# The sample group's expert unit in the middle of the sequence on 128 doubled rows, and the last four up-row groups using the free down-row buffers too

## What the reference computes

```
def block(xb):
    qv = (xb @ w_query).astype(f32).reshape(PEER_BLOCK, PEER_HEADS, 2, PEER_DHALF)
    s = jnp.einsum('thsd,hskd->thsk', qv, keys)
    sv, si = lax.top_k(s, PEER_TOPK)
    cand = sv[:, :, 0, :, None] + sv[:, :, 1, None, :]
    ...
    g = jax.nn.softmax(fv, axis=-1)
    u = expert_down[eidx]
    act = jax.nn.gelu(jnp.einsum('thkd,td->thk', u, xb).astype(f32), approximate=False) * g
    v = expert_up[eidx]
    return jnp.einsum('thk,thkd->td', act.astype(v.dtype), v)
```

## Time and profile before

| | us |
|---|---|
| Median of 3 runs | 2483.84 (2475.89 to 2489.05) |
| The profiled execution, its own time | 2482.62 |
| Its span | 2480.7 |
| GpSimd busy (1154 instructions) | 1090.3 (44%) |
| VectorE busy | 1510.9 (61%) |
| TensorE busy | 1365.7 (55%) |
| Mean granted TensorE clock | 0.733 of full speed |

### The profile page before, as it was taken

The page is one execution under the profiler, slowest core; times in us unless marked ns, Lnnn a source line. Parts: engine busy times, 40 slices in busy tenths (PEclk is TensorE's granted clock), DMA queues, the critical chain, the costliest instruction groups (busy, mean ns, idle before and its releaser), DMA issues.

```text
span 2480.7 us, 19709 instructions
## 1 busy us (share of the span) xinstructions
PE 1365.7 (55%) x6380; PEld 764.8 (31%) x6380; DVE 1510.9 (61%) x3235; ACT 279.0 (11%) x575; POOL 1090.3 (44%) x1154
## 2 busy tenths in 40 slices
PE   4697997999644998556652222233233233233265
PEld 0276674878633845443320000000000000000010
DVE  0454998165688123777667776767776767676411
ACT  1011000111112002111110110000110001010000
POOL 0122000010130000476767777777777777777632
PEclk7798998999766999787866666655656665665555
DMA  9821000221332050799999999999999999999854
GB/s 367 315 64 52 34 34 0 87 73 37 94 94 93 2 189 26 296 365 403 409 403 409 409 406 409 409 406 405 406 401 396 409 409 405 408 403 407 279 145 152
DMA packets 209033, 651.98 MB, mean 263 GB/s; under 512 B 26192, under 2 KB 52464, under 8 KB 204793
## 3 DMA queue, kind: packets, MB, share of 16 engines
q0 software_dynamic: 150016, 545.33, 56.6%
q1 hardware_dynamic: 58092, 103.70, 11.8%
q10 hardware_dynamic: 824, 1.70, 0.2%
HBM read 643.24 MB, written 7.54 MB: 262 GB/s over the span
## 4 chain that ended last, share of the span: by engine, by line
DMA 21%; POOL 15%; issue 10%; PE 7%; DVE 7%; DVEq 0%; POOLq 0%; ACT 0%
DMA arena<-in_expert_up_dram,rows 16%; POOL arena L1675 8%; POOL arena L1659 7%; DMA arena<-in_expert_down_dram,expert 5%; PE ps L1797 4%; DVE arena L1903 2%; PE ps L1805 2%; DVE arena L1862 0%; DVE arena L1861 0%; PE ps L1344 0%; DVEq L1855 0%; DVE keys L1860 0%; DVE arena L1888 0%; DVE arena L1885 0%; DVE arena L1889 0%
## 5 line engine op out<-in xcount | busy, mean ns | idle before, releaser
L1797 PE MATMUL ps<-arena 128*32 128x512 f32 x2048 | 409.8, 942 | 831.1 <-DMA arena<-in_expert_up_dram,rows 831.1
L1903 DVE CUSTOM_DVE_ANT_0 arena<-arena,ps 128x1024 f32<-128x1024 f32 x512 | 617.1, 1219 | 317.0 <-DMA arena<-in_expert_down_dram,expert 301.7
L1675 POOL DMA_INDIRECT arena<-in_expert_up_dram,rows x512 | 490.6, 958 | 241.0 <-issue 136.4
L1659 POOL DMA_INDIRECT arena<-in_expert_down_dram,expert x528 | 501.3, 949 | 200.8 <-issue 155.8
L1797 PEld LDWEIGHTS ps<-arena 128*32 128x32 f32 x2048 | 81.9, 146 | 1120.1 <-issue 1120.0
L546 PE MATMUL ps<-arena 128*128 128x260 f32 x896 | 207.7, 391 | 14.8 <-ACT arena L477 7.8
L546 PEld LDWEIGHTS ps<-arena 128*128 128x128 f32 x896 | 173.0, 194 | 52.3 <-issue 16.2
L954 POOL MEMSET arena<- 128x528 f32 x2 | 1.1, 538 | 305.2 <-POOLq L2017 305.2
L1344 PE MATMUL ps<-arena 128*128 128x260 f32 x512 | 124.4, 404 | 4.9 <-POOL counting L1642 3.4
L1071 PE MATMUL ps<-arena 128*128 128x260 f32 x512 | 112.5, 383 | 0.0
L1344 PEld LDWEIGHTS ps<-arena 128*128 128x128 f32 x512 | 102.0, 202 | 28.9 <-issue 6.3
(11 more groups left out here) (347 smaller groups left out, 1878.4 us busy)
## 6 DMA issues: line engine op xcount, KB each, us to landing
arena<-in_w_ada_dram SPq DMA_DIRECT2D x12, 2048.0 KB
arena<-in_w_in_dram SPq DMA_DIRECT2D x11, 2048.0 KB, 8.4
arena<-in_expert_down_dram,expert POOLq DMA_INDIRECT x528, 12.6
arena<-in_w_ada_final_dram SPq DMA_DIRECT2D x4, 2048.0 KB
arena<-in_w_query_dram SPq DMA_DIRECT2D x8, 1024.0 KB, 16.4
arena<-in_expert_up_dram,rows POOLq DMA_INDIRECT x512, 12.1
out_dram<-arena SPq DMA_DIRECT2D x13, 512.0 KB, 2.9
arena<-in_x_prompt_dram SPq DMA_DIRECT2D x2, 2048.0 KB
```

The lines of the kernel that those rows point to most:

```text
L1659: G.indirect_dma_start(U[i][0:rows, :], None, down, bass.IndirectOffsetOnAxis(ap=idx[u % 2][0:rows, k:k + 1], axis=0))\
L1675: G.indirect_dma_start(Vr[j], None, up, bass.IndirectOffsetOnAxis(ap=at, axis=0))\
L1797: last = mm(ps[32 * j:32 * j + 32, c, :], Z[:, j, m, :], Vr[4 * half + j][:, c * 512:(c + 1) * 512], start=(p % 4 == 0 and m == 0), stop=( ...
L1903: V.tensor_tensor_reduce(U[i][0:rows, :], U[i][0:rows, :], row, 1.0, 0.0, ALU.mult, ALU.add, dots[g % 2][0:rows, j:j + 1]).then_inc(s_uuse ...
```

## The change

The sample unit becomes one step of 128 rows: the partitions 0 to 63 hold the 64 sample rows with the experts 0 to 7, and the partitions 64 to 127 the same rows with the experts 8 to 15. For that its scores and its rows are made on all 128 partitions (twice the matmuls in `score_samples`, wider ones in `samples`), and top-k's result is copied into an index tile `sample` of its own in two halves. The add has 8 experts with a weight of 128 rows by 8 columns instead of 16 with 64 rows. The sample unit is put between the token units 19 and 20 (step 40 of now 65), and its closing three units later. The up buffers get a second set, the first eight down buffers: of the last four up groups (61 to 64) the second and the fourth use it, and the first of these waits until all products are done. The rest renumbers steps, waits and closings accordingly.

The core of the diff:

```diff
-            last = nc.tensor.matmul(ps[0:64, 2 + t % 2, 0:NK], self.qpad[:, t, :], self.kT[:, t, :], start=(t < 2),
-                                    stop=(t >= 2 * PH - 2))
+            for r in (0, 64):
+                last = nc.tensor.matmul(ps[r:r + 64, 2 + t % 2, 0:NK], self.qpad[:, t, :], self.kT[:, t, :],
+                                        start=(t < 2), stop=(t >= 2 * PH - 2))
...
-    Vr = rows16[0:VR]
+    S = 2 * NU
+    units = list(range(NU))
+    units.insert(20, "samples")
+    steps = [S if u == "samples" else 2 * u + half for u in units
+             for half in range(1 if u == "samples" else 2)]
+    NSTEP = len(steps)
+    step_of = {g: n for n, g in enumerate(steps)}
+    unit_at = {g: (units.index("samples") if g == S else units.index(g // 2)) for g in steps}
+
     first_U, all_U = rows16[VR:] + more, rows16[VR:] + more + late
+    Vr = [rows16[0:VR], all_U[0:VR]]
...
-    groups = [("token", v) for v in range(2 * NU)]
-    groups[2 * NU - 2:2 * NU - 2] = [("sample", 0), ("sample", 1)]
-    at_step = {g: [g - LAG] for g in range(LAG, NSTEP)}
+    second = [n for n in range(NSTEP) if n >= NSTEP - LAG and (n - (NSTEP - LAG)) % 2]
+    at_step = {n: [n - LAG] for n in range(LAG, NSTEP)}
     at_step[NSTEP - 1] = list(range(NSTEP - 1 - LAG, NSTEP))
-    block_done = [2 * (16 * b + 16) + (4 if b == NB - 1 else 0) for b in range(NB)]
-    samples_done = 2 * 2 * NU
+    V_of = [1 if n in second else 0 for n in range(NSTEP)]
+    V_use = [1 + sum(V_of[m] == V_of[n] for m in range(n)) for n in range(NSTEP)]
+    V_before = [max([m for m in range(n) if V_of[m] == V_of[n]], default=None) for n in range(NSTEP)]
+    block_done = [2 * (step_of[16 * b + 15] + 1) for b in range(NB)]
+    samples_done = 2 * (step_of[S] + 1)
+    close_at = {units.index(PH * (b + 1) + 2): b for b in range(NB - 1)}
+    close_at[units.index("samples") + 3] = NB
+    closings = [close_at[u] for u in sorted(close_at)] + [NB - 1]
...
-                    G.indirect_dma_start(U[i][0:rows, :], None, down,
-                                         bass.IndirectOffsetOnAxis(ap=idx[u % 2][0:rows, k:k + 1], axis=0))\
+                    at = idxS[:, j:j + 1] if g == S else idx[u % 2][:, k:k + 1]
+                    G.indirect_dma_start(U[i], None, down, bass.IndirectOffsetOnAxis(ap=at, axis=0))\
...
+                g, r = steps[n], V_of[n]
+                if g != S and g % 4 == 0:
+                    pool.wait_ge(s_idxT, g // 4 + 1)
+                    pool.sem_inc(s_gatep, 1)
+                if r and V_before[n] is None:
+                    pool.wait_ge(s_uused, GATE * NSTEP)
                     pool.sem_inc(s_gatep, 1)
                 for j in range(VR):
-                    if j % 4 == 0 and n:
-                        pool.wait_ge(s_vused, 2 * (n - 1) + 1 + j // 4)
+                    if j % 4 == 0 and V_before[n] is not None:
+                        pool.wait_ge(s_vused, 2 * V_before[n] + 1 + j // 4)
                         pool.sem_inc(s_gatep, 1)
...
-                            k = GATE * v + 4 * half + j
+                            k = 4 * half + j
                             pe.wait_ge(s_sd, k + 1)
                             for c in range(2):
-                                last = mm(ps[0:NS, 2 + c, :], sdiag[0:64, k, :],
-                                          Vr[4 * half + j][0:64, c * 512:(c + 1) * 512],
-                                          start=(k == 0), stop=(k == 2 * GATE - 1))
+                                last = mm(ps[0:NS, 2 + c, :], sdiag[:, k, :], Vr[r][k][:, c * 512:(c + 1) * 512],
+                                          start=(k == 0), stop=(k == GATE - 1))
                     last.then_inc(s_vused, 1)
...
-                for n in at_step.get(g, ()):
-                    add(n)
+                if n >= LAG:
+                    add(n - LAG)
+                if g == S:
+                    continue
...
+                if units[i] == "samples":
+                    V.tensor_copy(idxS[0:64, :], ef[0:64, 0:GATE])
+                    done(V.tensor_copy(idxS[64:P, :], ef[64:P, GATE:TOPK]))
+                    dve.sem_inc(s_top, 1)
+                else:
+                    V.tensor_copy(idx[par], ef).then_inc(s_top, 1)
...
+            for i, u in enumerate(units):
+                if u == "samples":
+                    products(step_of[S])
+                    topk(i + 1)
+                    weight(step_of[S])
+                    continue
+                n, b = step_of[2 * u], u // PH
...
+                c = close_at.get(i)
+                if c is not None:
+                    k, rows, r = closings.index(c), NS if c == NB else P, c // NB
+                    if c == NB:
+                        close(k, samples_done, ps[0:NS, 2:4, :], NS, 1, x1[0:NS, NB * D:(NB + 1) * D])
+                    else:
+                        close(k, block_done[c], ps[:, 0:2, :], P, 0, x1[:, c * D:(c + 1) * D])
+                if i + 1 < len(units):
+                    topk(i + 1)
...
-            for g in (2 * NU, 2 * NU + 1):
-                products(g)
-                weight(g)
-            close(3, samples_done, ps[0:NS, 2:4, :], NS, 1, x1[0:NS, NB * D:(NB + 1) * D])
-            variance(3, NS)
-            normed(3, NS, 1)
```

More of the change, by code:

```diff
@@ L1544, in stage_peer @@
     yb = take(D)
-    x64 = take(D)
+    xs = take(D)
     late = [take(D) for _ in range(2)]
@@ L1550, in stage_peer @@
     Z = take(4, 8, 32)
-    sel64 = take(PH, NS, rows=NS)
-    r64 = take(NS)
+    sel = take(2 * PH, NS, rows=NS)
+    pick = take(NS)
     s_rep = take(2, NK)
@@ L1566, in stage_peer @@
     gel = [take(GATE) for _ in range(2)]
[L1567 removed]
+    acts = take(GATE)
+    sdiag = take(GATE, NS)
     stat, rstd = take(1), take(1)
@@ L1783, in add @@
             def add(n):
-                kind, v = groups[n]
-                p = v // 4
-                if kind == "token" and v % 4 == 0:
+                g, r = steps[n], V_of[n]
+                p = g // 4
+                if g != S and g % 4 == 0:
                     pe.wait_ge(s_Z, 4 * p + 4)
-                if kind == "token" and v % 16 == 0 and v:
-                    pe.wait_ge(s_blkrd, v // 16)
+                if g != S and g % 16 == 0 and g:
+                    pe.wait_ge(s_blkrd, closings.index(g // 16 - 1) + 1)
                 for half in range(2):
                     for j in range(4):
-                        pe.wait_ge(s_V[4 * half + j], 16 * (n + 1))
-                    if kind == "token":
-                        m = 2 * (v % 4) + half
+                        pe.wait_ge(s_V[r][4 * half + j], 16 * V_use[n])
+                    if g != S:
+                        m = 2 * (g % 4) + half
                         for c in range(2):
@@ L1813, in samples @@
                 pe.wait_ge(s_ssrd, 2)
-                nc.tensor.transpose(ps[0:64, 4, 0:NS], sel64.rearrange("p h b -> p (h b)"), ident[0:NS, 0:NS])
+                rows = sel.rearrange("p h b -> p (h b)")
+                nc.tensor.transpose(ps[:, 4, 0:NS], rows, ident[0:NS, 0:NS])
                 for j in range(2):
-                    last = mm(ps[0:64, 2 + j, :], sel64.rearrange("p h b -> p (h b)"),
-                              h2[0:NS, 4 * D + j * 512:4 * D + (j + 1) * 512], start=True, stop=True)
-                last.then_inc(s_ps64, 1)
+                    last = mm(ps[:, 2 + j, :], rows, h2[0:NS, 4 * D + j * 512:4 * D + (j + 1) * 512],
+                              start=True, stop=True)
+                last.then_inc(s_psx, 1)
             ask(2)
-            for g in range(NSTEP):
+            for n, g in enumerate(steps):
                 u, p = g // 2, g // 4
@@ L1847, in _ @@
                     turned(actT, actb[p % 2]).then_inc(s_actT, 1)
+            for n in range(NSTEP - LAG, NSTEP):
+                add(n)
         @block.vector
@@ L1863, in top16, with topk @@
                 V.max_index(index[:, 8:16], vals[:, 8:16], rep)
-            def topk(unit):
-                par = unit % 2
-                ef = efb[(unit // 2) % 2][:, unit % 2, :]
+            def topk(i):
+                par, unit = i % 2, units[i]
+                ef = efb[0][:, 0, :] if unit == "samples" else efb[(unit // 2) % 2][:, unit % 2, :]
+                unit = NU if unit == "samples" else unit
                 for s in range(2):
@@ new lines, in weight @@
+            def weight(n):
+                g = steps[n]
+                par = unit_at[g] % 2
+                dve.wait_ge(s_gelu, n + 1)
+                if g == S:
+                    tt(acts[0:64, :], gel[n % 2][0:64, :], w[par][0:64, 0:GATE], ALU.mult)
+                    tt(acts[64:P, :], gel[n % 2][64:P, :], w[par][64:P, GATE:TOPK], ALU.mult).then_inc(s_acts, 1)
+                else:
+                    if g % 4 == 0 and g >= 8:
+                        dve.wait_ge(s_actT, g // 4 - 1)
+                    u, half = g // 2, slice((g % 2) * GATE, (g % 2 + 1) * GATE)
```

(14 more changed lines are left out.)

196 lines of the change are left out of this document (84 added, 112 removed).

## The result

The changed kernel takes **2419.56 us** in the median of four runs (2417.09 to 2422.96), the kernel before 2480.39 us beside it (four runs, 2475.89 to 2489.05). The ratio of the times is 0.9752, with a 95% interval of 0.9725 to 0.978: 2.5% faster. Forecast were 2416 us, 2404 to 2435. Two later measurements of the same kernel gave 2417.41 and 2419.15 us, five runs each. The forecast took its start from a median of 2483.84 us for the kernel before; beside the changed kernel it measured 2480.39. So the time is 3.6 us off, but the change, -60.8 us where -68.1 were forecast, is 7.3 us off: half of that error is hidden by the start.

A forecast was written before the change was run, and what follows sets the result against it. The prediction took the DMA to bound the middle, with a slower, serial end. Its terms, -176.8+20.6+81.6+6+0.5 = -68.1 us, took 2483.8 us to 2416 us, range 2404 to 2435.

The forecast's parts named there:

- term 1: The old end, from issue of the last token down-gather at 2303.9 to 2480.7, is removed: -176.8 us.
- X: At the new end: the moment when issue of the last down group ends, from which the end is counted.
- Term 2: In the DMA-bound middle: one more full step, 16 sample gathers of 128 rows instead of 32 of 64: +20.6 us.
- Term 4: Behind the sample step: GpSimd waits 12.5 us for top-k, the queue covers 6.5, DMA idles: +6 us (0 to 8.4).
- Term 5: Sample add in the middle: 32 records in 15.3 us as the clock rises, nearly all hidden by the queue: +0.5 us.
- term 3: New end: group 61 waits for group 60's add, then 32 gathers follow, last add and closing: +81.6 us.
- Rival B: Sample gathers: duplicate rows still run at half rate, 20.6 us more, 2436 us; chance 0.05.
- rival C: At the end: the second buffer set brings nothing, a group costs 13.9 us, 11 us more, 2427 us; chance 0.06.
- rival D: Later units: top-k stays late, GpSimd stalls before each of 11 units, slower than before, 2508 us; chance 0.03.
- The rule that the prediction weighed: TensorE's clock: sustained matmuls release the throttle, only idling brings it back, whatever the rows; sample add then costs 0.5 us.
- Rival A: Sample add: TensorE stays at 1.2 GHz, GpSimd waits 6.4 and 8.7 us, +11.6 us, 2427 us; chance 0.27.

The follow-up runs named there:

- the experiment with 64 partitions: Changed kernel with the 16 sample gathers, down and up, cut to the first 64 of their 128 partitions, half the bytes: 2426.97 us.
- the kernel with the short add: Changed kernel leaving out three of four experts in each half of the samples' add, all gathers kept: 2418.89 us.
- the 64 rows: Changed kernel whose samples' add uses only the first 64 of the 128 rows of each gathered tile: 2429.8 us.
- the one with top-k first: Changed kernel with top-k of the unit behind the samples moved ahead of the samples' products, its softmax ahead of the samples' gelu: 2412.49 us.

## Why the prediction was right, and where it was off

The mean of the three traces of each kernel, by the prediction's terms:

| Stretch | forecast | measured |
|---|---|---|
| tail removed (term 1) | -176.8 | -177.6 |
| from the end of down group 63 of before to X (terms 2, 4, 5) | +27.1 | +30.3 |
| X to the end (term 3) | +81.6 | +83.4 |
| sum | -68.1 | -63.9 |

**Term 1 and the bound** hold: up to the sample unit the middle is unchanged (group 16 to 40: 500.6, 500.5 and 500.3 us before, 500.5, 500.3 and 500.4 after), the tail with its half-rate gathers and its slow add is gone.

**Term 2** holds: 16 gathers of 128 partitions cost one step. The eight up-gathers of the samples run at 408 to 410 GB/s (1928 to 1936); where the down-gathers' bytes move, the rate falls to 316, which goes with VectorE's sample products (above). The prediction expected 409 in the whole sample step and put nothing for this; it is 1.6 us of bytes. Rival B is out by the rates of both kernels and by the experiment with 64 partitions.

**Term 3** is right by its steps, X+21.2 for group 61, then 32 gathers at the DMA's rate, and 1.8 us short in the mean (82.35, 84.2, 83.66). The "some 92 us" from the last down-gather to the end, in the prediction's list of what the profile would show, contradicts its own 81.6; it is nearly the figure of rival C (X+92.6), and measured are 82 to 84. The 32 gathers are issued from 2356.06 to 2394.56 and the add that needs the last begins at 2402.98, 46.9 us after the first one's start, where the forecast had 5.6+31x1.285 = 45.4 us. In the first trace that is partly made good by luck: the last add found the clock at 1.00 and took 1.92 us, not the 3.64 of the sum, while the closing took 12.3 and not 11.4.

**Term 4** has the reasoning that did not hold, and was priced a little low if anything. Its stall came at its place and in its size, 12.91 us against 12.5, and once; rival D is false, no later unit waits for top-k. What it costs was put at 6 us, with 8.4 as the upper bound, for which the prediction shows no working. Two readings of the price: the kernel with the short add has this stall and no wait for the add, and its middle, 517.0 us from down group 40 to X against 487.8 to the same point before, is 29.2 us longer; less the extra step of 20.6 and the 1.6 of bytes beside the sample products this leaves 7 us, give or take a scatter of 1 to 2. And taking the stall away gave 4.9 us by medians and 6.2 by traces, with an edit that loses up to 3.1 us of GpSimd's issue of its own, which makes it 5 to 9. The reasoning that failed is that the landing time of 12.1 us is the length of the queue, so that 6.5 us of the stall would be covered and the DMA would idle for 6. By the windows' shares 12 us is the queue of one engine of sixteen. The last gather ahead of the stall was issued at 1836.1 (1849.94-12.91-0.94); fifteen engines were empty some 6 us later, one only at 1847. From 1836 to 1860 the mean rate is 205 GB/s, 12 us of bytes less than 409 would give, while the one engine is empty for some 4 us. The measured price lies between, and the runs don't settle by what share.

**Term 5** holds. The clock rose, and did so for the reason that it was argued from, the rows: with 64 of them it stays at 0.50. The rule that the prediction weighed (the Trainium skill, TensorE: Matmul & The Clock Gate, Part 1) agrees with the trace for 128 rows and not for 64, where 27.46 us without a pause leave the clock at 0.50. Rival A was priced at +11.6 us, with waits of 6.4 and 8.7; brought about by the 64 rows it measured +10.65, with 8.02 and 8.99. The term itself, 0.5 us, measured 0.3 to 2.0, which is within the scatter. Its waits were 3.35 and 2.20 us where 0.4 and 1.9 were worked out: the fourth sample gather (its start 1923.9) let the add begin at 1933.31, 9.4 us later and not 8.1, the first half took 9 us and not 8.5, and the 0.8 us in which GpSimd wakes, counted in term 3, were left out here.

So of the 4.2 us between the forecast and the measured change of the span (means of the three traces), 3.2 lie in the middle, half of it in the bytes lost beside the sample products, for which there was no term, and the rest in terms 4 and 5, which the scatter does not let me part; 1.8 lie in the end, less 0.8 for the longer tail in one trace of before.

## What to carry to other kernels

A group of gathers that fills 128 partitions costs what one of 64 does, so work that was split over two half-filled steps is worth packing, and a serial tail is worth moving into a stretch that the DMA bounds. Before a spare buffer set is handed out, look for the first group that waits: here the same set, given one group earlier, was worth 5 to 7 us more. A stall of the issuing engine is covered for less than a gather's landing time of 12 us suggests: of the 12.9 us in front of down group 41 some 4 to 8 were free, at the samples' add most of the first 6.3, and there each further microsecond was a microsecond of time.

## What the runs showed of the hardware that I had not expected

- **One DMA engine runs behind the other fifteen.** Behind a stop of issue the share stays at about 0.06 (29 to 25 GB/s) for up to 5 us, in the changed kernel at 1842 to 1847, but for 0.11 in one of these, and at 2352 to 2356. The Trainium skill (DMA: Bandwidth & Descriptors, "Latency and other measured facts") says that two of the engines are usually slower than the others; the trace has no engine numbers, and its share is that of one.
- **Rows and the clock.** Matmuls of 128x8 weights take TensorE from 0.50 (1932 to 1936) to 1.00 (from 1940), those of 64x8 don't in 27.46 us, nor in the 54.77 of the earlier trace rows.
- **Gathers of 64 partitions delay others.** They run at 168 to 206 GB/s at a share of 1.03, and a 128-partition group that was asked for earlier (up group 35) was added 8.5 us later than in the changed kernel.
- **A gather's issue can double, and where VectorE's operands lie goes with it.** All 92 issues over 1.5 us (up to 1.99 instead of 0.94) end 0.8 us behind a VectorE instruction with SBUF operands alone; beside products that read PSUM none takes over 0.95 us. While the samples' products run, on SBUF alone, the DMA's rate falls too, to 316 GB/s in the changed kernel and 317 in the one with top-k first; why was not tried.
